# Encoder block on one core: which engine's DMA queue issues the reads of the down product's stored activation blocks

## What is computed

```python
gu = rmsnorm(h, g_ffn[i]) @ w_gate_up[i]
g_, u_ = gu[..., :D_FF], gu[..., D_FF:]
h = h + (jax.nn.silu(g_) * u_) @ w_down[i]        # D_MODEL = 2048, D_FF = 5632
```

## Time and profile before

| | us |
|---|---|
| median of 3 runs | 2655.09 (2654.67 to 2655.56) |
| the profiled execution's own time | 2658.29 |
| its span, first to last instruction | 2656.5 |
| pair 21 (ends the gate and up product) | about 1956.6 to 1997.2 |
| pair 22 | about 1997.2 to 2039 |
| pair 25 | about 2117 to 2158 |
| pair 29 | about 2276 to 2316 |

### The profile page before, as it was taken

One profiled execution on the slowest core, in us unless ns is written; L12 is line 12 of the kernel. 1 busy time (PEld: TensorE's weight loads), 2 busy tenths in 40 slices (PEclk: granted clock), 3 DMA queues, 4 the chain that ended last, 5 costly groups with the idle time before them and its releaser, 6 DMA issues. The chain is left out here.

```text
span 2656.5 us, 37937 instructions
## 1 busy us (share of the span) xinstructions
PE 2632.9 (99%) x14980; PEld 2309.0 (87%) x14980; DVE 2020.0 (76%) x2310; ACT 1286.2 (48%) x1612; POOL 179.1 (7%) x140
## 2 busy tenths in 40 slices
PE   9999999999999999999999999999999999999997
PEld 7989888888888888898888888888899898999887
DVE  7888767655565433488998999899899898888745
ACT  7545455434445233454554555554554453444543
POOL 0000000010000111100000000000000000000052
PEclk9999999999999999999999999999999999999999
DMA  7455323223333554446545555554666664643332
GB/s 247 139 160 163 127 87 95 79 88 112 107 94 108 182 208 124 146 126 180 165 143 177 172 153 167 175 151 151 177 210 216 190 224 126 208 137 106 94 103 96
DMA packets 137055, 392.75 MB, mean 148 GB/s; under 512 B 11584, under 2 KB 43456, under 8 KB 134336
## 3 DMA queue, kind: packets, MB, share of 16 engines
q1 hardware_dynamic: 121168, 342.27, 37.7%
q0 software_dynamic: 11232, 39.85, 8.5%
q10 hardware_dynamic: 4496, 8.44, 0.8%
HBM read 304.26 MB, written 46.40 MB: 132 GB/s over the span
## 5 line engine op out<-in xcount | busy, mean ns | idle before, releaser
L1290 ACT ACTIVATE w_hi<-raw 128x1024 fp32r<-128x1024 f32 (+1 forms) x539 | 563.3, 1046 | 756.8 <-PE ps L1203 408.3
L827 PE MATMUL ps<-arena,w_hi 128*128 128x512 f32 x2704 | 647.6, 391 | 1.3 <-DVE arena L2059 1.1
L827 PEld LDWEIGHTS ps<-arena,w_hi 128*128 128x128 f32 x2704 | 505.3, 188 | 109.9 <-issue 4.9
L1197 PE MATMUL ps<-arena,w_hi 128*128 128x512 f32 x1792 | 448.8, 392 | 0.5 <-DVE res L2742 0.5
L2554 DVE TENSOR_TENSOR w_lo<-raw,w_hi 128x1024 fp32r<-128x1024 f32 (+1 forms) x315 | 375.0, 1191 | 80.0 <-ACT w_hi L1290 78.3
L2005 DVE TENSOR_TENSOR w_lo<-raw,w_hi 128x1024 fp32r<-128x1024 f32 x172 | 219.3, 1275 | 233.3 <-ACT w_hi L1290 231.6
L1197 PEld LDWEIGHTS ps<-arena,w_hi 128*128 128x128 f32 x1792 | 322.3, 189 | 58.3 <-DVE res L2742 0.7
L1203 PEld LDWEIGHTS ps<-arena,w_lo 128*128 128x128 f32 x2468 | 332.3, 191 | 17.6
L1203 PE MATMUL ps<-arena,w_lo 128*128 128x256 f32 x2468 | 346.4, 282 | 0.0
L832 PE MATMUL ps<-arena,w_lo 128*128 128x512 f32 x1352 | 334.3, 389 | 0.0
L1290 ACT ACTIVATE hi<-raw 128x1024 fp32r<-128x1024 f32 (+1 forms) x183 | 190.4, 1041 | 250.8 <-PE ps L1203 208.2
(11 more groups left out here) (272 smaller groups left out, 3358.6 us busy)
## 6 DMA issues: line engine op xcount, KB each, us to landing
raw<-w_gu SPq DMA_DIRECT2D x174, 512.0 KB, 4.0
raw<-raw POOLq DMA_DIRECT2D x70, 512.0 KB, 7.9
raw<-w_in SPq DMA_DIRECT2D x68, 512.0 KB, 3.4
raw<-w_dn SPq DMA_DIRECT2D x64, 512.0 KB, 4.5
hid<-res SPq DMA_DIRECT2D x22, 1024.0 KB, 5.0
raw<-w_z SPq DMA_DIRECT2D x40, 512.0 KB, 5.0
raw<-w_o SPq DMA_DIRECT2D x32, 512.0 KB, 3.7
raw<-w_pg SPq DMA_DIRECT2D x32, 512.0 KB, 3.6
```

The lines of the kernel that those rows point to most:

```text
L827: mm(ps[:, bank + t, :], w_hi[:, s, t, k], x[:, part, :], start=first and k == 0 and part == 0, stop=False)
L1197: mm(parts, w, x[:, :, k], start=fresh and k == 0, stop=False, skip_group_check=not fresh)
L1290: return nc.scalar.activation(out, in_, ACT.Copy, scale=scale)
```

## The change

Fills 1 to 6 of each generation are no longer issued by SP. ScalarE issues them, in its main loop, after `hi(14q + t + 2)` at t = 2, 4, 6, 8, 10 and 12 of pairs 21, 25 and 29. Each has the same two waits as before, now on ScalarE. Fill 0 stays on SP, as `first_fill`. Sources, targets, sizes and semaphores of all 21 fills are the same.

```diff
+        HID_BLOCK = [0, 4, 7, 2, 6, 3, 5]
+        CHANGE = {first_unit(g) // 2 - 1: g for g in (1, 2, 3)}
...
-            def fill(g, j):
+            def first_fill(g):
                 sp.wait_ge(hid_out, 16 * min(8 * g, FF // 2))
-                if j:
-                    sp.wait_ge(s_used, order(first_unit(g) - 1, j - 1) + 1)
-                elif g == 1:
+                if g == 1:
...
-                g = {first_unit(g) // 2 - 1: g for g in (1, 2, 3)}.get(q)
                 more = b < UNITS
                 if more:
                     block_load(a, A21)
                     block_load(b, A21)
-                if g:
-                    fill(g, 1)
-                    fill(g, 2)
                 if more:
                     block_load(a, A22)
-                if g:
-                    fill(g, 3)
-                if more:
                     block_load(b, A22)
                     block_load(a, A11)
-                if g:
-                    fill(g, 4)
-                if more:
                     block_load(b, A11)
...
                     block_load(a, A12)
-                if g:
-                    fill(g, 5)
-                if more:
                     block_load(b, A12)
-                if g:
-                    fill(g, 6)
...
+            def fill(g, j):
+                act.wait_ge(hid_out, 16 * min(8 * g, FF // 2))
+                act.wait_ge(s_used, order(first_unit(g) - 1, j - 1) + 1)
+                n = 6 if g == 3 else 8
+                act.dma_start(x_slot(g, j)[:, 1].bitcast(F32),
+                              hid[g - 1, HID_BLOCK[j], :, 0:n, :]).then_inc(fill_in[j], 16)
...
                 for t in range(14):
                     if 14 * q + t + 2 < 7 * UNITS:
                         hi(14 * q + t + 2)
+                    if q in CHANGE and t in (2, 4, 6, 8, 10, 12):
+                        fill(CHANGE[q], t // 2)
                     if t == 1 and now:
```

More of the change, by code:

```diff
@@ L716, in hidden_store @@
                              res[:, 12:16, :].rearrange("p r (h c) -> p (r h) c", h=2)).then_inc(hid_out, 16)
-            HID_BLOCK = [0, 4, 7, 2, 6, 3, 5]
-            def fill(g, j):
+            def first_fill(g):
                 sp.wait_ge(hid_out, 16 * min(8 * g, FF // 2))
-                if j:
-                    sp.wait_ge(s_used, order(first_unit(g) - 1, j - 1) + 1)
-                elif g == 1:
+                if g == 1:
                     sp.wait_ge(xs_lo, 22)
@@ L729, in fill @@
                 n = 6 if g == 3 else 8
-                sp.dma_start(x_slot(g, j)[:, 1].bitcast(F32),
-                             hid[g - 1, HID_BLOCK[j], :, 0:n, :]).then_inc(fill_in[j], 16)
+                sp.dma_start(x_slot(g, 0)[:, 1].bitcast(F32),
+                             hid[g - 1, HID_BLOCK[0], :, 0:n, :]).then_inc(fill_in[0], 16)
             def residual_again(i):
@@ L785, in _ @@
                     if q == (10 if g == 1 else first_unit(g) // 2 - 2):
-                        fill(g, 0)
+                        first_fill(g)
                 if q == FF // 2 + 8:
```

## The result

The changed kernel takes 2660.18 us (median of 20 runs, 2658.19 to 2662.53), the kernel before 2655.35 us (20 runs, 2654.48 to 2656.49). The ratio is 1.0019, with an interval of 1.0012 to 1.0025: 4.8 us slower, and 1.2 us beyond the upper end of the range. The runs also scatter more, over 4.3 us in place of 2.0. The profiled execution took 2661.75 us with a span of 2659.8 us.

The account below looks back on a forecast made before the run. TensorE, busy for 99% of the span, was taken to bound the kernel. SP, ScalarE waits, issues and landing each came to 0, sum 0, so 2655.1 us against the median of 2655.09; range 2653.0 to 2659.0.

Parts of the forecast that it names:

- The waits of the fills: On ScalarE: each fill's waits, for s_used and for the stores, already met when reached; cost 0.
- The issues: 18 DMA issues added on ScalarE, 0.37 us each, 6.7 us in all, covered by its idle time; cost 0.
- SP's loads: Removing six issues in each of three pairs from SP leaves its loads at the same times; gain 0.
- No fill held up TensorE: Fills' new issue times: none becomes late; tightest is fill 1, landing at 1979.2 against 1981.
- The 1.0 and 0.5 us of pair 22: TensorE stalls in pair 22, put down to VectorE's backlog and expected to stay in the same place.
- rival B: Earlier weight landing shrinks TensorE's 1.0 and 0.5 us stalls in pair 22: faster, 2653.6 us; chance 0.07.
- What is moved: the bandwidth: Pairs 21 and 25: second unit's A11 load lands 3 us earlier or 3.3 us later; taken as 0.
- rival A: Second unit's A11 load 3.3 us late through contention in pairs 21 and 25: 4.5 us slower, 2659.6; chance 0.12.
- signs of being wrong: New TensorE wait in pair 22 or 26, VectorE idle near 1997, ACTq issues over 1.5 us, pair 22 under 40.5 us.
- The middle of two bounds: Pair 21's second A11 load, landing between 1992.8 and 1999.3; middle taken as inside the margins, 3.0 and 2.1 us: 0.
- The relief that I expected from an earlier fill 3: Fill 3 falls 1.8 us earlier, into a DMA gap, relieving the full stretch from 1978 by up to that much.
- The 2.3 us of pair 30: TensorE wait at 2347 to 2349.5 us after ScalarE's wait for a weight load; the change doesn't reach it.

Follow-up runs that it names:

- e10: Changed kernel with fill 4 issued at t = 12, fill 5 at t = 13, fill 6 in the next pair at t = 1, all from ScalarE: 2655.19 us.
- e7: Like e3, all fills from ScalarE at later places, but fill 4 kept at the changed kernel's t = 8: 2656.68 us.
- e3: Changed kernel with all six fills still from ScalarE but issued later, at t = 3, 5, 7, 9, 12, 13: 2655.39 us.
- e1: Changed kernel with fills 4 and 5 back on SP in their old places, fills 1, 2, 3, 6 still from ScalarE: 2656.48 us.
- e11: Changed kernel with only fills 4 and 5 moved later, to t = 9 and t = 12: 2655.82 us.

## Why the prediction was wrong

**Right.** The waits of the fills are met when ScalarE reaches them. The issues cost nothing (0.33 us each, at times when the engine is busy copying or idle anyway). SP's loads didn't move. No fill held up TensorE. The 1.0 and 0.5 us of pair 22 stayed. They stay in e10 too, where the second A11 load takes 6.7 us in place of 10.1 and ScalarE has no wait for it: they don't hang on ScalarE's late start, and rival B fell.

**The step that failed is the landing under "What is moved: the bandwidth", "I take 0".** In its place the two A11 loads of pair 21 took 11.9 and 12.3 us, not 5.6 and 10.1, those of pair 25 took 12.0 and 13.3 us, not 5.6 and 11.5, and the kernel lost 4.8 us. The kind of mechanism was rival A's: contention, an A11 load late, no spare time on VectorE. Of the signs of being wrong that I gave, its new waits of TensorE in pairs 22 and 26 came. Rival A had a chance of 0.12. That its 2659.6 us are so near the measured 2660.2 is partly luck: it had the second A11 load late by 3.3 us, which was to cost 3.3 us at the first seam and 1.2 at the second. The trace has the first load behind both stalls, 2.15 us of idle at the first seam, and 2.06 us with some 1.4 us of slow clock at the second (see the end). Three readings led away from it.

1. *Only one load was looked at.* The A11 load of the second unit was already late, so it drew the eye. The first A11 load wasn't in any wait row, as it had 3.5 us of slack, and both new stalls stand behind it. e7, with fill 4 alone early, shows ScalarE's new wait for it. My own time for fill 4 was 1982.0, and the trace has that load at 1982.36, where before fill 4 was behind it: the swap could be read off and wasn't priced.
2. *The margin was measured to the wrong consumer.* I counted 3.0 us from the second block's high part to the matmul that reads it. The nearer consumer was in VectorE's queue behind the first block's low part: the sum that frees the PSUM bank. Its margin was 0.05 us (1997.02 to 1997.07). So what was left of the first load's lateness after its slack and VectorE's other work showed in full.
3. *The issue times were too late.* I let a fill go out when ScalarE's copies ahead of it end. It goes out 0.1 us after the first of them begins: fill 4 at 1980.12 and not 1982.0, fill 5 at 1985.85 and not 1986.8. Both errors made the change look more harmless.

**The middle of two bounds was no estimate.** The lower bound, landing at 1992.8, rested on the second A11 load getting out from behind fill 4. It landed at about 1998.1, near the upper bound of 1999.3. I had said that this load took 10 us because it stood in one queue with fill 4. In e3 fill 4 is in another queue, and the load takes 10.2 us, against 10.1 before; in e10 fill 4 leaves later, and it takes 6.7. So it was the fill's bytes and not the shared queue. From the rule of packet turns (the Trainium skill, DMA: Bandwidth & Descriptors, Queues, rings and completion order) I had concluded that the loads get out early. That conclusion didn't come true. The rule itself is neither shown nor refuted, as none of these rows tells single packets apart. The relief that I expected from an earlier fill 3 can't be seen either: in e1 and e11 the second A11 load lands no sooner than before.

**The 2.3 us of pair 30** The earlier trace rows were chance. The changed kernel has 0.3 us there, and e1, e3 and e10 show 0.3 to 0.4. The profiled execution of before was 3.2 us above its median, and this stall with its slow clock is most of that. It makes the two profiles differ by 3.5 us (2658.29 and 2661.75) where the medians differ by 4.8.

## What to carry to other kernels

A DMA that is moved to another engine's queue changes its place in time against every transfer that runs beside it, and where the DMA engines were full, in these runs, that place counted and not the queue. Before moving one, list which loads it now precedes, and for each its margin to the nearest consumer, through the in-order queue of the engine that takes it, and not only to the matmul. Prefetches with much time to spare belong behind the loads with little.

## What the runs showed of the hardware

ScalarE issues a DMA while its copy runs: in the changed kernel the copy starts at 1980.01 and the issue behind it at 1980.12. It even leaves ahead of the half copy of 1980.98, which stands before it in the program (L1719, in `hi`).

A stall of 2 us can cost more than its length. Stretches of the changed kernel after the stall of 2.06 us (columns as in the earlier trace rows):

```profile
2160.00:2162.00 2.00, 0.61 (x6) 0.40 (x4) 1.97 (x4) 0.04 (x1) 0.00 (x0) 1.00 1.09 447
2162.00:2166.00 4.00, 3.33 (x16) 3.33 (x17) 3.57 (x5) 2.91 (x3) 0.00 (x0) 0.57 0.70 293
2166.00:2170.00 4.00, 4.00 (x36) 4.00 (x35) 2.72 (x4) 2.01 (x2) 0.00 (x0) 1.00 0.03 7
```

The granted clock is 0.57 in the second one, so most of it was at 1.2 GHz, and matmuls start 0.213 us apart there (16 of them) in place of 0.12: about 1.4 us lost. It doesn't follow every stall: after the 2.15 us of pair 22 in the same execution the clock stayed at 1.00. In the kernel before, 0.72 from 2348 to 2354 us came after the 2.3 us of pair 30. That some stalls draw this in and others don't would also widen the scatter of the runs; this was not tested apart.
